# A two-layer hybrid mixer on one core: narrow matmuls packed on TensorE, q's norms moved into the softmax scales, and RWKV's triangular levels with the second head on the anti-diagonal quarters

## The reference

```python
def reference(x, ...):
    for l in range(2):
        p = rms_norm(x, norm_g[l]) @ w_in[l]
        z, p_rw, p_ml, p_mla, p_da = _split(p, IN_WIDTHS)
        y_rw = rwkv7_group(p_rw, ...)       # 8 heads of 64, a recurrence over the tokens
        y_ml = mlstm_group(p_ml, ...)       # 4 heads of 128, chunks of 64 tokens, 4+4 gate columns
        y_mla = mla_group(p_mla, ...)       # 4 heads, q and k of 128 plain + 64 rotated columns
        y_da = diff_attn_group(p_da, ...)   # 4 heads, two softmaxes over 64 columns each
        y = concat(beta * mixers) * silu(z)
        x = x + y @ w_out[l]

def causal_attention_blocks(q, k, v, coeffs, scale):   # q and k are rms-normed first
    s = where(kpos <= qpos, einsum('bqhmd,bkhmd->bhmqk', q_blk, kf) * scale, neg)
    attn = einsum('m,bhmqk->bhqk', coeffs, softmax(s))
    return einsum('bhqk,bkhv->bqhv', attn, vf)

def _wkv7_scan(r, w, k, v, kk, a):                     # per head, state S 64 x 64
        sa = einsum('bhvk,bhk->bhv', S, -kk_t)
        S = S * w_t + sa * (kk_t * a_t) + v_t * k_t
        return S, einsum('bhvk,bhk->bhv', S, r_t)
```

## Time and profile before

| | |
|---|---|
| median of 3 runs | 2634.35 us (2631.59 to 2634.81) |
| the profiled execution | 2631.67 us, its span 2630.0 us |
| TensorE busy | 95% of the span, mean granted clock 0.979 |
| GpSimd, VectorE, ScalarE busy | 66%, 45%, 24% |
| moved by DMA | 290 MB, 110 GB/s in the mean |

### The profile page before, as it was taken

One profiled execution on the slowest core, in us unless ns is written; L12 is line 12 of the kernel. 1 busy time (PEld: TensorE's weight loads), 2 busy tenths in 40 slices (PEclk: granted clock), 3 DMA queues, 4 the chain that ended last, 5 costly groups with the idle time before them and its releaser, 6 DMA issues. The chain is left out here.

```text
span 2630.0 us, 39931 instructions
## 1 busy us (share of the span) xinstructions
PE 2491.1 (95%) x16064; PEld 1853.5 (70%) x16064; DVE 1181.4 (45%) x1650; ACT 640.1 (24%) x1109; POOL 1730.6 (66%) x1196
## 2 busy tenths in 40 slices
PE   5999999999999998999969999999999999988999
PEld 4866577777777776667858666777777777766677
DVE  4123236646555762344241222366476557633442
ACT  4222211212111122332232223112122112223322
POOL 2675578658558876677626655777576588766675
PEclk9999999999999998999979999999999999999999
DMA  6622243223224335522336232432232244355223
GB/s 204 183 80 81 80 129 117 77 78 105 78 70 140 116 117 177 168 77 68 119 87 181 80 96 61 149 102 82 70 108 78 69 140 131 103 178 170 77 67 121
DMA packets 158690, 290.18 MB, mean 110 GB/s; under 512 B 21648, under 2 KB 30224, under 8 KB 156896
## 3 DMA queue, kind: packets, MB, share of 16 engines
q1 hardware_dynamic: 108864, 187.09, 25.5%
q10 hardware_dynamic: 49632, 100.46, 10.8%
HBM read 235.57 MB, written 56.10 MB: 111 GB/s over the span
## 5 line engine op out<-in xcount | busy, mean ns | idle before, releaser
L735 POOL TENSOR_SCALAR w_hi<-raw 128x512 fp32r<-128x512 f32 x552 | 899.4, 1629 | 659.2 <-PE ps_proj L765 547.4
L740 POOL TENSOR_TENSOR w_lo<-raw,w_hi 128x512 fp32r<-128x512 f32 (+1 forms) x640 | 842.1, 1316 | 224.7 <-ACT w_hi L1186 178.5
L765 PE MATMUL ps_proj<-h_hi,w_hi 128*128 128x512 f32 x1760 | 730.9, 415 | 18.2 <-POOL w_lo L740 11.1
L765 PE MATMUL ps_proj<-h_hi,w_lo 128*128 128x512 f32 x1760 | 690.7, 392 | 0.0
L765 PE MATMUL ps_proj<-h_lo,w_hi 128*128 128x512 f32 x1760 | 689.4, 392 | 0.0
L765 PEld LDWEIGHTS ps_proj<-h_hi,w_hi 128*128 128x128 f32 x1760 | 332.5, 189 | 125.2 <-issue 31.4
L765 PEld LDWEIGHTS ps_proj<-h_lo,w_hi 128*128 128x128 f32 x1760 | 333.1, 189 | 71.9 <-issue 11.1
L765 PEld LDWEIGHTS ps_proj<-h_hi,w_lo 128*128 128x128 f32 x1760 | 332.3, 189 | 72.5
L780 PE MATMUL ps_proj<-w_hi,h_hi 128*128 128x512 f32 x448 | 184.8, 412 | 3.7 <-issue 3.7
L780 PE MATMUL ps_proj<-w_lo,h_hi 128*128 128x512 f32 x448 | 177.3, 396 | 0.0
L780 PE MATMUL ps_proj<-w_hi,h_lo 128*128 128x512 f32 x448 | 177.1, 395 | 0.0
(11 more groups left out here) (332 smaller groups left out, 3208.7 us busy)
## 6 DMA issues: line engine op xcount, KB each, us to landing
raw<-in_w_in_dram SPq DMA_DIRECT2D x480, 256.0 KB, 2.7
raw<-in_w_out_dram SPq DMA_DIRECT2D x128, 256.0 KB, 3.0
projected<-stage ACTq DMA_DIRECT2D x118, 256.0 KB, 2.9
arena<-projected ACTq DMA_DIRECT2D x90, 256.0 KB, 3.1
arena<-out_dram ACTq DMA_DIRECT2D x2, 4096.0 KB, 16.6
gated_hi<-arena ACTq DMA_DIRECT2D x24, 256.0 KB, 2.3
gated_lo<-arena ACTq DMA_DIRECT2D x24, 256.0 KB, 2.9
h_hi<-gated_hi SPq DMA_DIRECT2D x8, 768.0 KB, 6.8
```

Of the source, the lines that this page charges most:

```text
L735: nc.gpsimd.tensor_scalar(hi, src, 1.0, None, ALU.mult).then_inc(s_hi_split, 1)
L740: nc.gpsimd.tensor_tensor(lo, src, hi.bitcast(F32), ALU.subtract).then_inc(s_raw_split, 1)
L765: last = mm(ps_proj[:, m, :], lhsT, rhs, start=(k == 0 and j == 0), stop=(k == KT - 1 and j == 2))
```

## The change

On TensorE:

- Begin: the lambda product leaves the start and stands behind MLA's first sums. DVE makes the diagonal of the scales after the parameters instead of before, and ACT takes the first four high halves one by one between its copies of h instead of together after the fourth.
- `G_MISC`: mLSTM's gate columns are 32 wide. Their low half is put beside their high half in the same weight tile (columns 32 to 63), so the third tile takes two matmuls with 64 output rows in place of three.
- MLA: the rotated part of q is multiplied for two heads at once (128 output rows, in even heads only), and so is its rotation, on two diagonal quarters. The sum of squares of q is turned: q's squares are the stationary operand and one column of ones the moving one, which gives a sum per token on the partitions, in 4 matmuls of 1 column; the shares of the 64 rotated columns are added by DVE beforehand. q is no longer scaled: its inverse norm goes into the maxima's and the exponentials' scale.
- RWKV: the lora of v lies on rows 64 to 95 of the array instead of 0 to 31. In the levels, the second head's products go to the opposite partition half (input on one half, output on the other: the anti-diagonal quarters), alternating with the first head's, and one wait serves both heads. After the Gram stage a product with the identity and a fifth copy on ACT bring that head's matrix across; in the last level another identity product brings it back.
- mLSTM: the forget row is brought to partitions 64 to 67 by a DMA, and its product (L1073 before) takes 4 rows there in place of 36.
- Differential attention: q's sum of squares is turned as in MLA (4 matmuls of 2 columns), the scores of the two softmaxes stand side by side on the two row halves, and both masks come behind them.

Elsewhere: the table of fills has other numbers (among them 8 tiles before the first differential head moved to `da_first`, which has 17), the halves of y are loaded on SP's queue in four pieces from step 253 on, each behind a wait of its own, instead of all at step 265; the gates' logarithm on ACT moves from the second pair's transposes of v to its gate.

The diff, cut:

```diff
-begin=4, la_first=36, la_sums=17, la_v=4, la_heads=(7, 7, 7, 7), la_qk=(12, 12, 12, 12),
-la_probs=(11, 11, 13, 13), la_turned=(3, 3, 3, 3), la_gate=(4, 4, 4, 4),
-rw_first=8, rw_lora=(10, 9, 9, 9), rw_factors=(30, 34, 32, 31), rw_turned=(4, 4, 4, 4), rw_v=(2, 1, 1, 1),
+begin=4, la_first=36, la_sums=18, la_v=4, la_heads=(7, 7, 7, 7), la_qk=(12, 11, 12, 11),
+la_probs=(13, 13, 13, 13), la_turned=(3, 3, 3, 3), la_gate=(4, 4, 4, 4),
+rw_first=8, rw_lora=(10, 9, 9, 9), rw_factors=(31, 36, 36, 32), rw_turned=(4, 4, 4, 4), rw_v=(2, 2, 2, 2),
 rw_gram=(4, 4, 4, 4), rw_x=(2, 2, 2, 2), rw_level=(1, 1, 1, 1), rw_levels=(1, 1, 1, 1),
 rw_pu=(1, 1, 1, 1), rw_local=(5, 5, 5, 5), rw_state=(1, 1, 1, 1), rw_state_last=(1, 1, 1, 1),
-rw_carried=(2, 2, 2, 2), rw_mean=(3, 3, 3, 3), rw_gate=(12, 12, 14, 12),
-ml_first=28, ml_qk=(15, 12, 13, 13), ml_s=(8, 7, 6, 6), ml_h=(14, 14, 11, 11), ml_gate=(11, 12, 12, 12),
-da_first=4, da_sums=(16, 11, 11, 11), da_scores=(8, 5, 5, 5), da_half=(14, 12, 12, 12), da_turned=(0, 3, 3, 3),
-da_osq=(0, 9, 3, 3), da_gate=(8, 14, 14, 14))
+rw_carried=(2, 2, 2, 2), rw_mean=(3, 3, 3, 3), rw_gate=(13, 14, 13, 12),
+ml_first=27, ml_qk=(17, 10, 10, 10), ml_s=(8, 7, 7, 6), ml_h=(14, 14, 12, 11), ml_gate=(12, 12, 12, 12),
+da_first=17, da_sums=(16, 10, 10, 10), da_scores=(8, 6, 6, 6), da_half=(13, 15, 18, 18), da_turned=(3, 3, 3, 3),
+da_osq=(3, 4, 3, 3), da_gate=(9, 10, 10, 10))
...
-            sp.wait_ge(s_split_used, STEPS)
-            sp.wait_ge(s_y_kept, 32 * EARLY_K)
-        if 0 <= part < 4:
+        part, early = divmod(n - Y_LOADS, 3)
+        if 0 <= part < 4 and early == 0:
...
+            sp.wait_ge(s_split_used, STEPS - KT + 3 * part + 3)
...
+            gates = slice(2 * P, 2 * P + LANE)
+            lo_gates = w_hi[:, n % N_SPLIT, 2 * P + LANE:2 * P + 2 * LANE]
+            nc.gpsimd.tensor_tensor(lo_gates, src[:, gates], hi[:, gates].bitcast(F32), ALU.subtract)
...
+        if g == G_MISC and m == 2:
+            both = w1[:, 2 * P:2 * P + 2 * LANE]
+            rows, products = slice(0, 2 * LANE), ((both, h1), (both, h2))
         for j, (lhsT, rhs) in enumerate(products):
...
-    pe.wait_ge(s_lam_ready, 1)
-    mm(ps_proj[:, 1, 0:2], ones[0:64, :], lam_prod[0:64, :], start=True, stop=True
-       ).then_inc(s_da_lam_mm, 1)
...
+    for half in (slice(0, 64), slice(64, P)):
+        last = mm(ps[half, 2, :], rot_mla[half, :], la_peg[half, :], start=True, stop=True)
+    last.then_inc(s_la_sums, 1)
...
-        q0 = h * 192
         for j in range(3):
-            mm(ps[:, 0, :], la_wq[:, j, q0:q0 + P], la_in[:, j, :], start=(j == 0), stop=(j == 2))
-        for j in range(3):
-            mm(ps[0:64, 1, :], la_wq[:, j, q0 + P:q0 + 192], la_in[:, j, :],
-               start=(j == 0), stop=(j == 2))
...
+        own = slice(64 * (h % 2), 64 * (h % 2) + 64)
+        if h % 2 == 0:
+            for j in range(3):
+                mm(ps[:, 1, :], la_wq_pe[:, j, h * 64:h * 64 + P], la_in[:, j, :], start=(j == 0), stop=(j == 2))
...
         pe.wait_ge(s_la_heads_copied, h + 1)
-        mm(ps[:, 3, :], ones, la_hsq[:, 0, :], start=True, stop=False)
-        mm(ps[:, 3, :], ones[0:64, :], la_hsq[0:64, 1, :], start=False, stop=True)
-        mm(ps[:, 0, :], ones, la_hsq[:, 2, :], start=True, stop=False)
-        mm(ps[:, 0, :], ones[0:64, :], la_pesq[0:64, :], start=False, stop=True)
-        mm(ps[0:64, 1, :], rot_mla[0:64, :], la_qp[0:64, :], start=True, stop=True
-           ).then_inc(s_la_heads_sums, 1)
+        pe.wait_ge(s_la_squared, 2 * h + 2)
+        mm(ps[:, 0, :], ones, la_hsq[:, 2, :], start=True, stop=True)
+        pe.wait_ge(s_la_squared, 2 * h + 3)
+        for i in range(NT):
+            qs = slice(i * P, (i + 1) * P)
+            last = mm(ps[:, 3, i:i + 1], la_hsq[:, 0, qs], ones[:, 0:1], start=True, stop=True)
+        last.then_inc(s_la_sums, 1)
+        if h % 2 == 0:
+            for half in (slice(0, 64), slice(64, P)):
+                last = mm(ps[half, 1, :], rot_mla[half, :], la_qp[half, :], start=True, stop=True)
+            last.then_inc(s_la_turned_pe, 1)
         fill("la_qk", h)
-        pe.wait_ge(s_la_qk_ready, h + 1)
+        pe.wait_ge(s_la_scaled, h + 2)
         for i in range(NT):
             qs, ks = slice(i * P, (i + 1) * P), slice(0, (i + 1) * P)
             mm(ps[:, i, ks], la_q[:, qs], la_k[:, ks], start=True, stop=False)
-            mm(ps[:, i, ks], la_qp[0:64, qs], la_kp[0:64, ks], start=False, stop=False)
...
+            for i in range(NT):
+                own = slice(i * 64, (i + 1) * 64)
+                for q, o in swapped:
+                    mm(ps[q, 0, own], rw_gb[q, i, 0:64], rw_x[q, i, :], start=True, stop=True)
+                    last = mm(ps[o, 2, own], rw_gb[q, 4 + i, 0:64], rw_x[q, 4 + i, :],
+                              start=True, stop=True)
+            last.then_inc(s_rw_levelled, 1)
...
+            if lv:
+                pe.wait_ge(s_rw_xt_stepped, n_levels * hp + lv)
...
+                    fed = slice(256 + i * 64, 256 + (i + 1) * 64)
+                    for q, o in swapped:
+                        mm(ps[q, 0, fed], rw_xt[q, i, :], rw_y[q, i, :], start=True, stop=True)
+                        last = mm(ps[o, 2, fed], rw_xt[q, 4 + i, :], rw_y[q, 4 + i, :],
+                                  start=True, stop=True)
+                last.then_inc(s_rw_x_mm, 1)
...
+                    for q, o in swapped:
+                        mm(ps[q, 1, own], rw_y[q, i, :], rw_xt[q, i, :], start=True, stop=True)
+                        mm(ps[o, 3, own], ident[q, q], rw_xt[q, 4 + i, :], start=True, stop=False)
+                        last = mm(ps[o, 3, own], rw_y[q, 4 + i, :], rw_xt[q, 4 + i, :],
+                                  start=False, stop=True)
...
-        mm(ps[:, 1, :], sel_f[0:36, h * P:(h + 1) * P], ml_gt[0:36, :], start=True, stop=True
+        mm(ps[:, 1, :], sel_f[64:68, h * P:(h + 1) * P], ml_gt[64:68, :], start=True, stop=True
...
-        mm(ps[:, 0, :], bones, da_sq[:, 0, :], start=True, stop=True)
         mm(ps[:, 1, :], bones, da_sq[:, 1, :], start=True, stop=True)
+        for i in range(NT):
+            last = mm(ps[:, 0, 2 * i:2 * i + 2], da_sq[:, 0, i * P:(i + 1) * P], bones[:, 0:P:64], start=True, stop=True)
+        last.then_inc(s_da_sums, 1)
...
                     mm(ps[:, b, ks], da_g[half, 0, qs], da_g[half, 1, ks], start=True, stop=False)
-                    last = mm(ps[:, b, qs], mask_ident, neg, start=False, stop=True)
+                for m in range(2):
+                    last = mm(ps[:, 2 * (i % 2) + m, qs], mask_ident, neg, start=False, stop=True)
             last.then_inc(s_da_scores_mm, 1)
...
-        if k == 3:
-            for n in range(N_SPLIT):
-                high_part(n)
+        if k < N_SPLIT:
+            high_part(k)
...
-        if hp == 1:
-            act.wait_ge(s_ml_gate_abs, 1)
-            link(nc.scalar.activation(ml_sg[32:36, :], ml_sg[32:36, :], ACT.Exp, scale=-1.0))
-            nc.scalar.activation(ml_sg[32:36, :], ml_sg[32:36, :], ACT.Ln, bias=1.0).then_inc(s_ml_gate_log, 1)
...
+        if hp == 2:
+            act.wait_ge(s_ml_gates, 1)
+            act.dma_start(ml_gt[64:68, :], ml_gt[32:36, :]).then_inc(s_ml_gate_loaded, 16)
...
+    fill("to_z_da")
     square_qk(0)
-    fill("to_z_da")
...
-    dve.wait_ge(s_x_mean, 1)
-    v.tensor_tensor(rs_diag, ident[:, None, :].to_broadcast([P, NT, P]), rs_x[:, :, None].to_broadcast([P, NT, P]), MUL).then_inc(s_rs_diag, 1)
...
+    dve.wait_ge(s_x_mean, 1)
...
+        link(v.tensor_scalar(la_rq, la_rq, 192.0 ** -0.5, None, MUL))
+        link(v.tensor_tensor(la_kp[own, :], la_per[own, :], la_rsk[own, :], MUL))
...
-        row_maxima(la_mx, [(i, i) for i in range(NT)], 192.0 ** -0.5).then_inc(s_row_max, 1)
+        row_maxima(la_mx, [(i, i) for i in range(NT)], la_rq).then_inc(s_row_max, 1)
...
-            for h in range(2):
-                dve.wait_ge(s_rw_levelled, 2 * (n_levels * hp + lv) + h + 1)
-                v.tensor_tensor(rw_y[:, 4 * h:4 * h + 4, :], ps[:, 2 * h, 0:256].rearrange(by_chunk_rows, i=NT), level_mask, MUL).then_inc(s_rw_level_masked, 1)
...
+            y0, y1 = rw_y[:, 0:4, :], rw_y[:, 4:8, :]
+            m0, m1 = (ps[:, b, 0:256].rearrange(by_chunk_rows, i=NT) for b in (0, 2))
+            dve.wait_ge(s_rw_levelled, n_levels * hp + lv + 1)
+            link(v.tensor_tensor(y0, m0, level_mask, MUL))
+            v.scalar_tensor_tensor(out=y1, in0=m1, scalar=1.0 if lv < n_levels - 1 else -1.0, in1=level_mask, op0=MUL, op1=MUL).then_inc(s_rw_level_masked, 1)
...
-        v.tensor_tensor(da_g, da_g, da_rs, MUL).then_inc(s_da_qk_ready, 1)
+        link(v.tensor_scalar(da_rq, da_rq, 64.0 ** -0.5, None, MUL))
+        v.tensor_tensor(da_g[:, 1, :], da_g[:, 1, :], da_rsk, MUL).then_inc(s_da_qk_ready, 1)
```

More of the change, by code:

```diff
@@ L78 @@
 N_RAW, N_SPLIT = 6, 4
+Y_LOADS = STEPS - KT + 3 + N_RAW + N_SPLIT
 def tiles_of(g):
@@ L170, in rotation @@
         return m
-    put("rot_mla", rotation(64, 32, 64))
```

(28 more changed lines are left out.)

237 lines of the change are left out of this document (136 added, 101 removed).

## The result

The changed kernel takes 2497.26 us in the median of 4 runs (2490.75 to 2501.91), the kernel before 2634.58 (2631.59 to 2635.3): a ratio of 0.9484, 95% interval 0.9465 to 0.9504, 5.2% faster. The forecast was 2466, in a range from 2438 to 2508. The profiled execution is the one of 2498.22 us with a span of 2496.5, 133.5 less than before.

What follows compares the result with a forecast made beforehand. TensorE, busy 95% of the span, was taken as the bound. Nine terms, a to i, summed to 167.6 us off 2631.67, giving 2464.1, or 2466 us as a median; range 2438 to 2508, own range 2450 to 2485.

Steps and rivals of the forecast that it cites:

- the waits move: Rival: fills tuned to old durations, so half the waits' gain and half the clock's stay out; 2504 us, chance 0.17.
- a starts: Layer starts: transposes run earlier and high halves follow each copy of h; 7.7 us a layer, 15.4 us saved.
- b gate columns: Gate columns' weight tile: 32 matmuls of 512 columns go, less a cost for tile-size changes; 2.5 us saved.
- c MLA: MLA heads: rotated q for two heads at once and turned sums of squares; 31.7 us saved, 27 to 34.
- e levels: RWKV levels: four quarters shorten each level from 3.89 to 3.6 to 3.7 us, DVE setting the pace; 2.8 us saved.
- f mLSTM: mLSTM gate products: the 4-row forget product runs beside the 36-row one; 7.7 us saved, or 0.
- g differential: Differential attention: score pairs overlap, masks follow masks, less the turned sum's cost; 24.4 us saved.
- h waits: TensorE's waits in the mixers: 83.0 us fall to 27.5 through the new fills; 55.5 us saved.
- i clock: TensorE's clock: fewer waits and shorter starts mean less time at 1.2 GHz; 20 us saved, 8 to 35.
- the rival I had given 0.26: A change of tile size empties the array, so the mLSTM gate products don't overlap; 2474 us, chance 0.26.
- Rival 4: Packs don't overlap: pairs on two row halves with one output half share their way out; 2507 us, chance 0.08.
- The slow rival: RWKV's levels become short bursts whose pauses drop TensorE's clock; 2666 us, chance 0.04.

Runs made afterwards that it cites:

- e5: Changed kernel with 26 of its projection tiles at other places, the same number in all: 2463.49 us.
- e9: e5 with a 36-row mLSTM forget product, four tiles moved from pair 2's factors to pair 1's, pair 1's tanh and gate logarithm ahead of its gate's evacuations: 2442.78 us.
- e6: Changed kernel with the whole table of fills of the kernel before: 2555.71 us.
- e3: Changed kernel with RWKV's second head back on the diagonal quarters, waits still merged, no identity products or fifth copy: 2530.23 us.

## Why the prediction was right, and where it was off

The sign held and most of the size: of 168 us forecast, 133.5 came in the profiled execution. But the time lies outside my own range (2450 to 2485), 31 us above the forecast and 7 below the rival "the waits move" (2504); the wider range holds it because it took that rival in. Two of the signs I had named did not come: a list of waits under 60 us (it is 91.4) and a clock near 0.99 (0.982). And the sum has errors of both signs. By its own letters (the slots are those of the changed kernel's trace, the last column what each run above gave up):

| term | forecast | after, by slots of the trace | undone on the chip |
|---|---|---|---|
| a starts | 15.4 | 8.4 + 3.75 = 12.2 | 7.5 |
| b gate columns | 2.5 | 32 x 0.193 = 6.2 | |
| c MLA | 31.7 | 13.1 + 23.2 - 0.6 = 35.7 | |
| d lora | 7.6 | 8 x 0.85 = 6.8 | 5.6 |
| e levels | 2.8 | 40 x 0.46 - 2.3 = 16 | 12.1 |
| f mLSTM | 7.7 | 8 x (1.91 - 2.11) = -1.6 | |
| g differential | 24.4 | 8 x 3.33 - 0.7 = 25.9 | 27.4 (scores) |
| h waits | 55.5 | 83.0 - 53.1 = 29.9 | 58 (whole table, with its clock) |
| i clock | 20 | 2630 x 0.021 - 2496.5 x 0.018 = 10.3 | |

The slots of after are taken at 2.4 GHz here; with h and i they add to 141.4, 8 more than the 133.5 of the span. Gaps too short for the list grew by about 7 us, and part of them stands in the levels' slots already, so I don't close the sum further.

**f failed, by the rival I had given 0.26.** The step took the overlap of L918 and L919, two products of 32 rows, over to one of 36 beside one of 4. The rival's mechanism is what the trace shows, and it costs 0.2 a pair besides. The Trainium skill, TensorEngine Tiling (Array Packing), Key Properties, states that changing the tiling mode, not just the tile, drains the TensorE. The gate products agree: 2.11 us with unlike sizes, 1.91 and in series with equal sizes on the same rows, 1.06 with equal sizes on different rows. The gate columns don't show it as a cost: the change from 128 to 64 output rows of the array and back holds 0.47 us for two products of 512 columns, where two others hold 0.46. So what a change costs has to be measured for each kind. Rival 4, no overlap on different rows, is out for equal sizes.

**h was too bold, by half.** "L765 behind ACT's evacuation (17.4) goes" and "the other 31.4 keep 12" rested on reading causes one at a time. The rival "the waits move" named the size (28 us missing; 55.5 - 29.9 = 25.6 were). In e5 and e9, though, the waits give way to a handful of tiles each: they were not held by a chain but by numbers that fit other durations. The clearest is L942: the last four tiles of a group of 16 steps ended inside pair 1's gate, so ACT made four evacuations, 1.06 us apart, ahead of the tanh (L1256) for which DVE and then TensorE waited:

```profile
586.36 0.60 ACT L1225 ACTIVATE stage<-ps_proj 128x512 f32<-128x512 f32 x1 [4.31 <-PE ps_proj L785]
...
590.58 0.63 ACT L1256 ACTIVATE arena<-arena 128x512 f32<-128x512 f32 x1 [0.46 <-ACT stage L1225]
...
591.31 1.34 DVE L1587 SCALAR_TENSOR_TENSOR arena<-arena 128x512 f32<-128x512 f32 x1 [6.08 <-ACT arena L1256]
...
593.49 1.22 PE L942 MATMUL ps<-arena 32*128 32x512 f32 x1 [4.45 <-DVE arena L1594]
```

I had followed where groups of steps end for two places and not for all of them. L924's wait I expected to rise to 11; it fell to 5.7. And L785's wait for ACT's stage is 7.8 with the new table and 8.0 with the old one (e6), so it fell from 17.4 without the two groups of steps that I had named as the reason.

**i followed h**: half the waits left, half the clock's gain.

**e was mis-sized, by its hand-overs.** I put two hand-overs of 0.4 on DVE's 2.8 and got 3.6 to 3.7. (Against 3.89 that is 0.19 to 0.29 a level, and not the 0.17 to 0.2 that I went on with; the mean before was 3.85.) The ring is 3.39, by the starts in DVE's rows 0.46 + 0.42 + 0.82 idle + 0.90 + 0.45 + 0.34. The hand-over behind the subtractions is hidden, since L1006 needs only the first two of them. That DVE paces the levels holds only just: in the level shown, TensorE's last L1007 ends at 1674.96, 0.06 us before DVE's next mask, so both ways round are about as long, and in e3, where TensorE's is longer, DVE waits for it. My upper bound, 3.3, was nearer than my choice. **b and c** came out better than priced. In b I had priced the change of tile size by the mask's slot of 0.16 us, and the 0.47 above shows that this slot was no measure for it. In c a one-column product holds 0.105 us an instruction, not 0.131; and my sum there is 31.2 and not 31.7, since I had not taken off the 0.5 for the lambda product.

The slow rival never came near: no stretch at 1.2 GHz in the profiled execution has its start in the levels, though they are short bursts; TensorE waits 0.1 us at a time there.

Left open: what the load of y in four pieces gave was not tried by itself (the wait for it, L1138's 3.2 us in the list of before, is gone), nor which edit on ACT took half of L785's wait for the stage away under the old table.

## What to carry to other kernels

Before packing small matmuls, look at the shapes of the neighbours, not only at their rows: in this kernel equal sizes on different rows overlap in full, 36 beside 4 rows is slower than no packing (2.11 us against 1.91), and padding the smaller with zero rows turns one into the other. When products get shorter, the tiles that were laid out to hide other engines' work must be laid out anew, here worth 58 us of 137, and once more 34 to 45 after that; read the list of waits, find for each the one instruction that is late and what stands ahead of it on its engine, and ask of every group that ends what its evacuations delay. Price a wait of 2 to 3 us on TensorE at more than its length: here two waits of 1.8 us cost 9.0.
